# A decoder step's input projection: 21 weight tiles for 23, with the rope key columns spread by a 0/1 product

## The chip, the cores and the metric

The kernel runs on one core of a Trainium2 chip. The metric is the device time of one execution in microseconds; three runs are given for the kernel before, and their median counts. A profile of one execution stands beside them. The engines are TensorE (PE; its weight loads are PEld), VectorE (DVE), ScalarE (ACT), GpSimd (POOL) and SyncE (SP); an engine's name with a q is its queue of DMA issues.

## The reference, cut to what matters

The reference is one inference step of a two-layer hybrid decoder over 512 prompt tokens and 32 sample tokens (8 sequences of 4), 544 columns in all. Each layer begins with one combined projection, whose columns are split among three kinds of heads:

```python
proj = x @ lw["w_in"]                     # (544, 1024) @ (1024, 2680)
(z, xbc, dt_raw, q_raw, k_raw, v_raw, r_raw, g_lr, cq, ckv, kr) = jnp.split(proj, ...)
...
log_a = jax.nn.log_sigmoid(g_lr @ lw["gla_gate_w"] + lw["gla_gate_b"]) / GLA_TAU
...
x1, x2 = kr[..., :16], kr[..., 16:]
k_rope = concatenate([x1 * cos - x2 * sin, x1 * sin + x2 * cos])
```

Widths: z 512, xbc 1024, dt 8, q and k 128 each, v and r 256 each, the gate rows g_lr 16, cq 192, ckv 128 and the rope keys kr 32. Behind the projection come the state-space heads (SSD), the gated linear attention (GLA), the latent attention (MLA, the only one to use kr), the output projection, a norm, the feed-forward part and a second norm.

## The kernel before, in words

Everything is kept transposed: features on the 128 partitions, the 544 tokens along the row, split into two halves of 272 columns (HALF) because a PSUM bank holds 512 numbers. The layers are a hardware loop over L (line 499); inside it each stage is a block with one instruction list per engine, and a block ends with a barrier of all engines.

The change lies in the first block, the input projection (lines 500 to 692). Its weights come from HBM in loads of up to 256 columns of w_in into a ring of four slots (RING); PROJ_LOADS (lines 251 to 259) lists the pieces of each of 12 loads, PROJ_TILES (lines 261 to 270) cuts them into 23 tiles of 128 columns, in the order in which TensorE takes them: 12 tiles of z and xbc, 6 of q, k, v and r, then the first 128 columns of cq, ckv, the rope keys four times over (J_KR), the rope keys with their halves swapped four times over (J_KS), and last a mixed tile (J_MISC): the other 64 columns of cq, a block of 32 from C_DT on and a block of 32 from C_G on, of which the first 8 and the first 16 are wanted. The two key tiles are one load of twelve pieces, the mixed tile one of three.

Weights and activations are split into a high part (rounded to fp32r) and a low part (the rest), and a product is w_high x_high + w_high x_low + w_low x_high: 8 blocks of rows x 3 x 2 halves = 48 products a tile (split_product, lines 336 to 346). For tile i ScalarE rounds the weights (high_weights, line 320), GpSimd subtracts (low_weights, line 324), TensorE multiplies into one of three pairs of PSUM banks (line 343), and ScalarE copies the result to proj (line 641) or, for xbc, to the convolution's rows (lines 634 to 638). ScalarE's order is written out (lines 628 to 653): wait for product i, round tile i + 2, copy tile i; VectorE and ScalarE do the convolution beside it. On TensorE, line 587 puts the transposes of the parameter rows behind tile 3 and line 589 those of a small weight behind tile 8.

After the last tile TensorE waits for all copies (line 592) and transposes the convolution's last rows (lines 593 to 602); ScalarE copies them (lines 655 to 662), SP stores them and starts four w_out loads (lines 557 to 564), and the block ends.

SP's order in the block: two ring loads, 16 rows of parameters, the third ring load, small weights (lines 536 to 551; the gate's weight gw is line 539), the fourth, then the others, each when the product that last used its slot is done (slot_free, lines 309 to 312).

Later users: the SSD block transposes dt out of rows 64 to 95 of the mixed tile (line 748), the GLA block multiplies gw by the 16 gate rows (line 1134, two halves, K = 16), the MLA block squares and scales the cq rows and multiplies the keys by cos and the swapped keys by sin (lines 1541, 1588, 1589, 1595). mlaw, where gw lies, is written over by the low weights of later stages in every layer.

The constants are one host-made array (const_layout, host_constants), loaded once at the start (line 426). Its sel has, for each of four heads, a 0/1 matrix that spreads 32 rows to four groups of 32.

## Time and profile before

| | us |
|---|---|
| median of 3 runs | 2667.15 |
| lowest, highest run | 2656.22, 2682.72 |
| span of the profiled execution, first to last instruction | 2667.4 |
| its mean granted TensorE clock | 0.844 |

The profiled execution has no other time than its span; the span is 0.25 us over the median of the runs. In the rows, a start time counts from the span's first instruction. A row of the timeline has start, duration, engine, line, operation, written tile <- read tiles, shapes, and x the number of instructions merged; in brackets is the time for which the engine had been idle before it and what ended that. A granted clock of 1.00 is the upper of TensorE's two levels (2.4 GHz), 0.50 the lower (1.2 GHz).

### The profile page before, as it was taken

To read this page: it belongs to the slowest core of one execution; us is meant where nothing else is said; L and a number is where in the kernel's file an instruction comes from. 1 tells how busy PE (TensorE), PEld (TensorE's weight loads), DVE (VectorE), ACT (ScalarE), POOL (GpSimd) and SP (SyncE) were. 2 spreads that over 40 slices of the span, in tenths; PEclk is the share of its full clock that TensorE was granted. 3 is DMA by queue.
4 is the path that set the end of the run, shared out by engine and by line. 5 is a ranking of instruction groups with operands and counts; after the bars stand their busy time and mean duration, and the time that the engine had idled before them with its cause. 6 is when DMAs were issued, how large, how long until landed. Compare 5 with 4: busy or idle time off the path is not lost. (4 is left out here: it accounts for less than half of the span.)

```text
span 2667.4 us, 38846 instructions
## 1 busy us (share of the span) xinstructions
PE 2310.9 (87%) x16043; PEld 2092.2 (78%) x16043; DVE 916.7 (34%) x1506; ACT 813.8 (31%) x1471; POOL 657.1 (25%) x332
## 2 busy tenths in 40 slices
PE   4996677899987999989969785688998989999896
PEld 3995363498977999989859763446997889999896
DVE  2415562211123243335425067421111314343453
ACT  4322323222214222233344232323221232222334
POOL 0332040000022234334323223200000323434341
PEclk7997565778788999999989875657797999999998
DMA  3323102022111232222033301201230102222220
GB/s 109 106 40 97 40 5 84 7 73 96 63 36 41 79 96 94 77 84 88 24 109 80 104 5 36 84 6 40 80 119 4 64 31 90 95 94 95 66 80 34
DMA packets 168754, 177.14 MB, mean 66 GB/s; under 512 B 47199, under 2 KB 151303, under 8 KB 166341
## 3 DMA queue, kind: packets, MB, share of 16 engines
q1 hardware_dynamic: 163884, 132.51, 16.3%
q0 software_dynamic: 4608, 41.95, 4.3%
q8 instruction: 111, 1.82, 0.3%
q10 hardware_dynamic: 100, 0.46, 0.1%
q14 instruction: 51, 0.41, 0.1%
HBM read 166.04 MB, written 8.86 MB: 66 GB/s over the span
## 5 line engine op out<-in xcount | busy, mean ns | idle before, releaser
L324 POOL TENSOR_TENSOR w_low<-ring,w_high 128x1024 fp32r<-128x1024 f32 x120 | 291.2, 2427 | 678.2 <-ACT w_high L320 678.2
L343 PE MATMUL ps<-x_high,w_high 128*128 128x272 f32 x1664 | 347.0, 290 | 28.3 <-DVE x_low L334 22.3
L343 PE MATMUL ps<-x_high,w_low 128*128 128x272 f32 x1664 | 346.0, 289 | 0.0
L343 PE MATMUL ps<-x_low,w_high 128*128 128x272 f32 x1664 | 345.7, 289 | 0.0
L320 ACT ACTIVATE w_high<-ring 128x1024 fp32r<-128x1024 f32 x166 | 174.8, 1055 | 544.5 <-PE ps L343 489.2
L343 PEld LDWEIGHTS ps<-x_high,w_high 128*128 128x128 f32 x1664 | 262.8, 190 | 30.0 <-DVE x_low L334 23.2
L343 PEld LDWEIGHTS ps<-x_high,w_low 128*128 128x128 f32 x1664 | 262.4, 189 | 0.0
L343 PEld LDWEIGHTS ps<-x_low,w_high 128*128 128x128 f32 x1664 | 262.3, 189 | 0.0
L343 PE MATMUL ps<-x_high_in,w_high 128*128 128x272 f32 x736 | 154.3, 291 | 45.5 <-POOL w_low_in L324 45.5
L2183 DVE TENSOR_SCALAR arena<-arena,parb 128x560 f32<-128x560 f32 x44 | 84.6, 1922 | 277.3 <-ACT arena L2131 277.3
L1708 PE MATMUL ps<-xc 128*128 128x16 f32 x1024 | 176.6, 308 | 0.6
L324 POOL TENSOR_TENSOR w_low_in<-ring,w_high 128x1024 fp32r<-128x1024 f32 x46 | 109.9, 2390 | 271.7 <-ACT w_high L320 271.7
L1708 PEld LDWEIGHTS ps<-xc 128*128 128x128 f32 x1024 | 172.4, 254 | 2.3 <-ACT xc L1799 2.3
L2271 DVE TENSOR_TENSOR hidden_low<-big,hidden_high 128x544 fp32r<-128x544 f32 x88 | 122.1, 1394 | 138.5 <-ACT hidden_high L2238 138.5
L2258 PE MATMUL ps<-hidden_high,w_high 128*128 128x272 f32 x704 | 148.1, 292 | 12.7 <-DVE hidden_low L2271 11.9
L2245 POOL TENSOR_TENSOR w_low<-ring,w_high 128x512 fp32r<-128x512 f32 x88 | 117.3, 1336 | 169.2 <-ACT w_high L2237 169.2
L343 PEld LDWEIGHTS ps<-x_high_in,w_high 128*128 128x128 f32 x736 | 117.0, 190 | 46.5 <-POOL w_low_in L324 46.4
L343 PE MATMUL ps<-x_high_in,w_low_in 128*128 128x272 f32 x736 | 153.4, 290 | 0.0
L343 PE MATMUL ps<-x_low_in,w_high 128*128 128x272 f32 x736 | 152.9, 290 | 0.0
L2258 PE MATMUL ps<-hidden_low,w_high 128*128 128x272 f32 x704 | 147.5, 291 | 0.0
L2258 PE MATMUL ps<-hidden_high,w_low 128*128 128x272 f32 x704 | 147.1, 290 | 0.0
L2258 PEld LDWEIGHTS ps<-hidden_high,w_high 128*128 128x128 f32 x704 | 112.7, 192 | 13.6 <-POOL w_low L2245 12.5
(376 smaller groups left out, 3959.8 us busy)
## 6 DMA issues: line engine op xcount, KB each, us to landing
ring<-in_ffn_w_up SPq DMA_DIRECT2D x44, 1024.0 KB, 5.3
ring<-in_ffn_w_down SPq DMA_DIRECT2D x20, 1024.0 KB, 5.1
ring<-in_w_in SPq DMA_DIRECT2D x18, 1024.0 KB, 5.4
ring<-in_w_out SPq DMA_DIRECT2D x8, 1024.0 KB, 9.0
ring<-in_ple_w_gate SPq DMA_DIRECT2D x8, 1024.0 KB, 5.0
big<-in_state_ssm SPq DMA_DIRECT2D x16, 256.0 KB, 5.1
out_ssm_sample<-big SPq DMA_DIRECT2D x4, 1024.0 KB
arena<-in_x_prompt SPq DMA_DIRECT2D x1, 2048.0 KB
```

The costliest lines, as they stand in the source:

```text
L320: act.activation(wh[:, i % 2], ring[:, n % RING, :, c0:c0 + P], ACT.Copy).then_inc(s_high, 1)
L324: pool.tensor_tensor(low[:, i % 2], ring[:, n % RING, :, c0:c0 + P], wh[:, i % 2].bitcast(F32), ALU.subtract).then_inc(s_low, 1)
L343: last = pe.matmul(ps[:, b + h, 0:HALF], w[:, i % 2, k, :], x[:, k, h * HALF:(h + 1) * HALF], start=(k == 0 and x is x_high and w is wh), ...
L1708: last = pe.matmul(ps[:, sb_, 16 * t:16 * t + 16], kvT[:, n % 4, q * P:(q + 1) * P], qls[:, b].rearrange("p h l -> p (h l)"), start=False, ...
L2183: dve.tensor_scalar(c2, ab[:, i, 0:AO], pcol(0), pcol(3), ALU.mult, ALU.add)
L2245: pool.tensor_tensor(wld[:, s % 4], down_slot(LD_DOWN + i)[:, r_], whd[:, s % 4].bitcast(F32), ALU.subtract).then_inc(s_wl, 1)
L2258: last = pe.matmul(ps[:, 2 * m + h, 0:HALF], w[:, s % 4, m * P:(m + 1) * P], x[:, s % 4, h * HALF:(h + 1) * HALF], start=(k == 0 and w is ...
L2271: dve.tensor_tensor(hl[:, s % 4], hT[:, k], hh[:, s % 4].bitcast(F32), ALU.subtract).then_inc(s_hl, 1)
```

## The change

The rope key columns are loaded once, as rows 96 to 127 of the mixed tile. The two key tiles are gone; in their place a float32 product of a 32-row 0/1 matrix with these rows writes them four times over (matrix: sel for head 3) and swapped four times over (matrix: a new constant, kswap) into PSUM, and ScalarE copies them to the places where they were. The mixed tile moves ahead of the cq and ckv tiles; the first spread product stands behind the cq tile's product, the second behind the last one. The gate rows move from row 96 to row 72, which is no start for a product's rows, so that the gate product takes rows 64 to 95 and its weight has zeros for the rows that aren't gate rows: VectorE zeroes 32 rows of the weight, and SP's load of it waits for that.

```diff
-M_DT, M_G = 64, 96
+M_DT, M_G, M_KR = 64, 72, 96
...
-              ("eps_rms", 1), ("quarter", 1), ("blk64", 128), ("mean", 128), ("pgsel", 128)]
+              ("eps_rms", 1), ("quarter", 1), ("blk64", 128), ("mean", 128), ("pgsel", 128), ("kswap", 128)]
...
+    kswap = np.zeros((P, P), np.float32)
+    for rep in range(4):
+        for d in range(RD):
+            kswap[M_KR + (d + RD // 2) % RD, 32 * rep + d] = 1.0
+    put("kswap", kswap)
...
+        PROJ_LOADS.append([(0, C_CQ + 128, 64), (M_DT, C_DT, 8), (M_G, C_G, 16), (M_G + 16, C_G, 8),
+                           (M_KR, C_KR, RD)])
         PROJ_LOADS.append([(0, C_CQ, 128), (128, C_CKV, 128)])
-        PROJ_LOADS.append([(32 * r, C_KR, 32) for r in range(4)]
-                          + [(128 + 32 * r + 16 * h, C_KR + 16 * (1 - h), 16) for r in range(4) for h in range(2)])
-        PROJ_LOADS.append([(0, C_CQ + 128, 64), (64, C_DT, 32), (96, C_G, 32)])
...
-        PROJ_TILES += [(9, 0, 128, "c", J_CQ), (9, 128, 128, "c", J_CKV), (10, 0, 128, "c", J_KR),
-                       (10, 128, 128, "c", J_KS), (11, 0, 128, "c", J_MISC)]
+        PROJ_TILES += [(9, 0, 128, "c", J_MISC), (10, 0, 128, "c", J_CQ), (10, 128, 128, "c", J_CKV)]
...
-        N_IN, LD_OUT, LD_GATE, LD_PROJ, LD_UP, LD_DOWN = 12, 12, 16, 20, 21, 43
+        N_IN, LD_OUT, LD_GATE, LD_PROJ, LD_UP, LD_DOWN = 11, 11, 15, 19, 20, 42
...
-        gw = mlaw[M_G:M_G + 16, 1792:1920]
+        gw = mlaw[M_DT:M_DT + 32, 1792:1920]
...
-                    e.dma_start(gw, a["gla_gate_w"][L]).then_inc(s_w, 16)
+                    e.wait_ge(s_gz, 1)
+                    e.dma_start(mlaw[M_G:M_G + 16, 1792:1920], a["gla_gate_w"][L]).then_inc(s_w, 16)
...
+                    def spread_rope_keys(swapped):
+
+                        e.wait_ge(s_kept, N_PROJ - 2)
+                        by = C("kswap") if swapped else sel[:, 3, :]
+                        for h in range(2):
+                            last = pe.matmul(ps[:, (6, 0)[swapped] + h, 0:HALF], by[M_KR:M_KR + RD, :],
+                                             proj[M_KR:M_KR + RD, J_MISC, h * HALF:(h + 1) * HALF],
+                                             start=True, stop=True)
+                        last.then_inc(s_rep, 1)
...
                         if i == 8:
                             transposed_uk()
+                        if i >= N_PROJ - 2:
+                            spread_rope_keys(i - (N_PROJ - 2))
 
                     e.wait_ge(s_kept, N_PROJ)
+                    e.wait_ge(s_repk, 2)
...
+                        if i >= N_PROJ - 2:
+                            swapped = i - (N_PROJ - 2)
+                            e.wait_ge(s_rep, swapped + 1)
+                            act.activation(two(proj[:, (J_KR, J_KS)[swapped]]), halves((6, 0)[swapped]), ACT.Copy
+                                           ).then_inc(s_repk, 1)
...
                 @block.vector
                 def _(e):
+                    dve.memset(gw, 0.0).then_inc(s_gz, 1)
                     low_x(e, xl_in, xT, xh_in, s_xh, s_xl)
...
-                        last = pe.matmul(ps[:, h, 0:HALF], gw, proj[M_G:M_G + 16, J_MISC, h * HALF:(h + 1) * HALF],
+                        last = pe.matmul(ps[:, h, 0:HALF], gw, proj[M_DT:M_DT + 32, J_MISC, h * HALF:(h + 1) * HALF],
                                          start=True, stop=True)
```

## Rows read from the trace of the kernel before

**Rows 1.** The page, busy time of each engine (share of the span) x instructions.

```profile
PE 2310.9 (87%) x16043; PEld 2092.2 (78%) x16043; DVE 916.7 (34%) x1506; ACT 813.8 (31%) x1471; POOL 657.1 (25%) x332
```

**Rows 2.** Line 343 on TensorE, projection of each layer: from:to, length, busy, clock, DMA share, GB/s; one group.

```profile
63.10:204.20 141.10, 140.54 (x1104) 0.99 0.32 77
1366.30:1507.70 141.40, 140.85 (x1104) 0.99 0.31 76
...
L343 PE MATMUL ps<-x_high_in,w_low_in 128*128 128x272 f32 x736 | 153.4, 290 | 0.0
```

**Rows 3.** Timeline of ScalarE and GpSimd in the last tiles of layer 0's projection.

```profile
168.15 1.06 ACT L320 ACTIVATE w_high<-ring 128x1024 fp32r<-128x1024 f32 x1 [4.44 <-PE ps L343]
...
180.18 1.06 ACT L320 ACTIVATE w_high<-ring 128x1024 fp32r<-128x1024 f32 x1 [4.44 <-PE ps L343]
...
186.19 1.06 ACT L320 ACTIVATE w_high<-ring 128x1024 fp32r<-128x1024 f32 x1 [4.44 <-PE ps L343]
187.16 0.61 ACT L641 ACTIVATE big<-ps 128x544 f32<-128x544 f32 x1
187.33 2.39 POOL L324 TENSOR_TENSOR w_low_in<-ring,w_high 128x1024 fp32r<-128x1024 f32 x1 [3.62 <-ACT w_high L320]
...
192.20 1.06 ACT L320 ACTIVATE w_high<-ring 128x1024 fp32r<-128x1024 f32 x1 [4.44 <-PE ps L343]
```

**Rows 4.** Timeline of the end of layer 0's projection, to the next block's first product.

```profile
203.78 0.41 PE L343 MATMUL ps<-x_high_in,w_low_in 128*128 128x272 f32 x2
204.23 0.62 ACT L641 ACTIVATE big<-ps 128x544 f32<-128x544 f32 x1 [5.38 <-PE ps L343]
204.90 0.74 PEld L594 LDWEIGHTS ps<-cst,big 128*3 128x3 f32 x8 [0.93 <-ACT big L641]
...
209.07 5.49 SPq L245 DMA_DIRECT2D ring<-in_w_out  x4
...
215.01 0.66 PE L748 MATMUL ps<-cst,big 32*128 32x32 f32 x5 [8.20 <-PEq L512]
```

**Rows 5.** Float32 products of 272 columns: a group over the whole span, and a timeline row.

```profile
L2009 PE MATMUL ps<-big,ring 128*128 128x272 f32 x128 | 29.7, 392 | 0.0
...
313.45 2.15 PE L1134 MATMUL ps<-big,mlaw 16*128 16x272 f32 x4 [6.13 <-PEq L728]
```

**Rows 6.** SP's issues of the twelve-piece load, and slices: from:to, length, clock, DMA share, GB/s.

```profile
150.24 1.82 SPq L245 DMA_DIRECT2D ring<-in_w_in  x3
...
140.00:143.00 3.00, 1.00 1.12 306
...
158.00:161.00 3.00, 1.00 0.93 81
161.00:164.00 3.00, 1.00 0.44 51
```

**Rows 7.** Timeline of layer 0's start: VectorE's first work, SP's load of the gate weight.

```profile
54.54 5.17 DVE L334 TENSOR_TENSOR x_low_in<-xT,x_high_in 128x544 fp32r<-128x544 f32 x8 [3.37 <-ACT x_high_in L329]
...
64.45 0.33 SPq L539 DMA_DIRECT2D mlaw<-in_gla_gate_w  x1
```

**Rows 8.** The constants' load (KB, median us to landing), and TensorE's first work in the timeline.

```profile
cst<-in_consts SPq DMA_DIRECT2D x1, 1695.5 KB, 7.0
...
13.74 6.65 PE L459 MATMUL ps<-cst,arena 128*128 128x128 f32 x40 [13.74 <-DMA arena<-in_x_sample]
```

**Rows 9.** Timeline, the same two points in layer 0 and in layer 1.

```profile
63.11 0.82 PE L343 MATMUL ps<-x_high_in,w_high 128*128 128x272 f32 x2 [20.39 <-POOL w_low_in L324]
...
1344.77 5.62 ACT L414 ACTIVATE xT<-xT,par 128x544 f32<-128x544 f32 x8 [0.85 <-DVE xT L393]
...
1366.31 0.82 PE L343 MATMUL ps<-x_high_in,w_high 128*128 128x272 f32 x2 [25.14 <-POOL w_low_in L324]
...
2649.15 5.62 ACT L414 ACTIVATE xT<-xT,par 128x544 f32<-128x544 f32 x8 [0.85 <-DVE xT L393]
```

More of the change, by code:

```diff
@@ L509, in build @@
             craw = arena[:, 4096:4288].rearrange("p (k r) -> p k r", k=KD)
-            s_craw = sem("convrows_packed")
+            s_craw, s_gz = sem("convrows_packed"), sem("gate_rows_zeroed")
+            s_rep, s_repk = sem("rope_keys_spread"), sem("rope_keys_spread_kept")
             s_wh, s_wl, s_xh, s_xl = (sem(f"in_{n}") for n in ("w_high", "w_low", "x_high", "x_low"))
```

## The prediction

> **What bounds the kernel now.** I read the share of each engine first, then the projection stage by itself, then its last microseconds, and last the queues that feed it. TensorE is busy for 87% of the span and every other engine for 34% or less [rows 1], but the share is a mean over stages, so what a weight tile is worth has to be read where the tiles stand. In the input projection TensorE is busy for 140.54 of 141.10 us in layer 0 and 140.85 of 141.40 us in layer 1, at a granted clock of 0.99 [rows 2], that is, at the upper of its two levels for all but the first microseconds. The row of the products has a mean of 290 ns for one [rows 2]; that is no step, since neighbours overlap. The step is read from who waits for whom: ScalarE starts to round tile after tile at 180.18, 186.19 and 192.20 us, 6.01 us apart, and each time had sat idle 4.44 us until a product was done; its copy out of PSUM (0.61 us) and GpSimd's 2.39 us for the low part both end long before the next tile is asked for [rows 3]. So one tile is 48 products in 6.01 us (125 ns each), and here TensorE alone sets the pace.
>
> The end of the stage is a chain: the last product ends at about 204.19 us, ScalarE copies it (204.23 to 204.85), TensorE starts the transposes of the convolution rows at 204.90, ScalarE copies these, SP then sends four w_out loads from 209.07 for 5.49 us, and only behind the stage's barrier does TensorE go on, at 215.01 [rows 4]. What lengthens the time from the last product to the first transpose lengthens the kernel.
>
> **The change, part by part.** The sum is made against the profiled span, 2667.4 us; the median of the three runs is 2667.15, 0.25 below it, and the same difference is taken from it.
>
> *Two tiles fewer.* 96 products, two weight roundings, two subtractions and two copies go in each of two layers. Their ScalarE and GpSimd work lies beside TensorE now, so its going is worth nothing by itself; the gain is TensorE's: 4 x 6.01 = 24.04 us. The tiles in question are the ones rounded at 180.18 and 186.19 us, and their step is that of the others [rows 3]. After their going the next thing late is still TensorE: ScalarE's and GpSimd's chain for a tile is 1.06 + 2.39 = 3.45 us of the 6.01.
>
> *The first spread product* (two halves) stands between the products of the last two tiles. It waits for the mixed tile's copy, which is in PSUM one whole tile (6.01 us) earlier and takes 0.61 us, so the wait is over on arrival. Queued behind it on TensorE is the last tile's product: its price is a full addition. One float32 product of 272 columns is two records. The nearest row is the float32 product of the gate projection of the embeddings, 128 records in 29.7 us at the full clock, 0.232 us a record [rows 5]; four records make 0.93 us. Upper bound: the gate product of 16 rows, four records in 2.15 us, at the lower clock [rows 5]. Lower bound: two products at the projection's own 125 ns, 0.25 us. I take 0.93, since the row has the same kind, columns and clock; it has 128 rows in place of 32, and the 16-row one shows no gain from fewer rows (2.15 us at half the clock would be 1.08 at the full one). Its copy by ScalarE (0.61 us) lies in ScalarE's 4.44 us of idle time and costs nothing; if that cover were gone it would cost 0.61 a layer.
>
> *The second spread product* follows the last tile and waits for nothing that is late, as the same copy serves it. It is on the chain of the stage's end: 0.93 us of product, then 0.04 us to ScalarE, 0.61 us of copy and 0.05 us to the transposes make 1.63 us after the last product, where the copy and the transposes take 204.90 - 204.19 = 0.71 now. The last tile's own copy (0.62 us) lies beside the product. Added: 0.92 us a layer; bounds 0.25 and 2.15 by the same rows. Behind the new wait on the two copies stand the transposes, ScalarE's copies, SP's stores and four loads, and everybody at the barrier: it is paid in full.
>
> *The loads.* The twelve-piece load (keys and swapped keys) and the three-piece one go, a five-piece one comes. SP issues the twelve pieces from 150.24 us, and the traffic behind them has fallen off in the slice that ends at 164; in between it was 81 GB/s in 158 to 161 us, beside 306 in 140 to 143 us for a tile with rows of 1 KB [rows 6]. So twelve small pieces took about 12 us and held nobody, and five take an estimated 5. The new load takes the place of the one in rows 6 that ran at 140 to 143 us, so it can start at about 138 (product 12 frees its slot), and its first tile is rounded at 168.15 [rows 3]: 30 us, 25 of them to spare. Cost nothing.
>
> *Zeroing of the gate's rows.* VectorE clears 32 x 128 ahead of the low parts, while it waits for ScalarE's first rounding until 54.54 us; SP gets to the gate's load at 64.45, ten microseconds behind [rows 7]. Behind this wait on SP stand the small weights and the ring's fourth load. Nothing, unless the clearing came ten microseconds late. The gate's product has 32 rows in place of 16 at the same columns: nothing, by the rows of 16 and of 128.
>
> *Constants.* 128 more columns are 64 KB on top of 1695.5 KB that land in 7.0 us; TensorE starts at 13.74 us behind x, on the same queue [rows 8]. In proportion that is 7.0 x 64 / 1695.5 = 0.26 us, at the 306 GB/s of rows 6 0.21; I take 0.2, with 0 and 0.3 as ends.
>
> Sum: -24.04 + 2 x (0.93 + 0.92) + 0.2 = -20.1 us. By the low bounds -23.0, by the high ones -24.04 + 8.6 + 0.3 = -15.2. Forecast 2667.15 - 20.1 = **2647.0 us**, 0.75% less. A measurement of this kernel can tell about 1% from no change, so this comes out as within 1%, faster.
>
> **The rivals.**
>
> *The scatter or the later stages carry it over 1%.* The runs of before lie from 2656.22 to 2682.72, 10.9 below and 15.6 above the median, and nothing in the program differs between them. For it: both layers run the same instructions, and the time from the first projection product to the last bias of the second norm is 1344.77 - 63.11 = 1281.66 in layer 0 and 2649.15 - 1366.31 = 1282.84 in layer 1 [rows 9], so the same work at another moment moves by 1.2 us inside one execution, and by more between executions. Against it: that is small beside what is wanted, and has no sign. A draw as low as the lowest of before gives 2647.0 - 10.9 = 2636, below the bound of 2640.5. The Trainium skill (TensorE: Matmul & The Clock Gate, section "What's actually happening") says that the moment at which the clock rises is not tied to the kernel and differs from run to run. By that rule alone each later stage may gain or lose a little when it is moved forward; the 1.2 us of rows 9 agree with an effect of that size.
>
> *The spread goes the slow way.* If the four records run at the lower level of the clock or the copies at the end line up behind one another, both spreads cost 2.15 us each and the copy 0.61 on top: -24.04 + 2 x (4.3 + 0.6) + 0.3 = -13.9, so 2653. For it: the only float32 product with few rows in the trace is that slow [rows 5]. Against it: there TensorE had been idle for six microseconds, here it comes from 120 us at the full clock.
>
> *The mixed tile's load is late, and the change is a loss.* The mixed tile comes three tiles before the end and its five pieces are rows of 32 to 256 bytes; if they land late, ScalarE cannot round the tile and TensorE stands. It begins to cost when the five pieces take more than 30 us and undoes the whole gain at 30 + 10 = 40 us in each layer; at 46 us the kernel would be 2 x 6 = 12 us slower, 2679. Against it: twelve such pieces took 12 us [rows 6]. The Trainium skill (DMA: Bandwidth & Descriptors, the table at its head) states that a transfer of under 512 bytes is written by read-modify-write, which speaks against cutting a load so; by that rule all five pieces would be slow, as rows 6 agree (81 GB/s beside 306), and it still doesn't reach 30 us.
>
> *The stage isn't TensorE's.* If the loads or GpSimd set the step, two tiles fewer would give nothing: 2667 + 4 = 2671. Rows 3 exclude it almost wholly.
>
> **How the numbers follow.** Forecast as worked out, with its bounds 2644 to 2652: 0.63. Carried past 1%: 0.25. Slow spread: 0.07. Late load: 0.03. No gain: 0.02. The forecast's own band widened by the runs' scatter gives low 2636 (the second case's time) and high 2660 (2647 plus most of the 15.6 above the median); about 2 in 10 is left out. Faster by over 1%: 0.25. Slower by over 1%: the late load, 0.03. Within 1%: the rest, 0.72.
>
> **What would show it.** In the profile after, ScalarE's roundings stay 6.01 us apart and number 21 a layer; the first projection product to the last tile's copy is shorter by 2 x 6.01 - 0.93 = 11.1 us; that copy's start to the first conv-row transpose grows from 0.67 to about 1.6 us; the transposes to the next stage's first product stay at 10.1 us; the later stages keep their lengths within a microsecond or two. Wrong would be: a gap at the mixed tile with a DMA as releaser, four spread records taking over 1.2 us, a copy out of PSUM that starts more than 0.1 us behind its product, or a later stage that takes back several microseconds.

## The result, and the profile after

The kernel after takes 2634.86 us in the median of twelve runs (2622.99 to 2648.93). The kernel before, run beside it twelve times, takes 2655.03 us (2640.60 to 2682.72); the ratio is 0.9922 [0.9897, 0.9947]. Ratios and intervals, here and below, leave out runs of more than 1.5% above the fastest of the same kernel; medians and ranges hold all runs. That is 20.2 us less (0.78%), where 20.1 were forecast, and yet the time itself lies 12.1 us below the forecast 2647.0 and 1.1 below the low end 2636.0. Both have to be explained: why the difference came out, and why the level did not.

The profiled execution after spans 2636.7 us, 30.7 less than the one before. The page's share of each engine, to be read beside [rows 1]:

```profile
PE 2278.1 (86%) x15867; PEld 2055.1 (78%) x15867; DVE 917.3 (35%) x1508; ACT 810.4 (31%) x1467; POOL 647.5 (25%) x328
```

The counts are those of the change: TensorE has 176 products fewer (two layers of 96 less 8 of the spreads), GpSimd four subtractions fewer, VectorE two clears more. Next the timeline of layer 0: its start, then the last two tiles and the end of the projection (start, duration, engine, line; in brackets the idle time before and what ended it). After the change L323 rounds weights, L346 is the projection's product, L592 the spread, L659 the tile copy, L668 the spread's copy, L612 the first conv-row transpose, L250 SP's loads and L772 the next block's first product.

```profile
13.58 2.79 PE L462 MATMUL ps<-cst,arena 128*128 128x128 f32 x12 [13.58 <-DMA arena<-in_x_sample]
...
53.91 0.17 DVE L697 MEMSET mlaw<- 32x128 f32 x1 [2.71 <-PEq L172]
54.57 5.17 DVE L337 TENSOR_TENSOR x_low_in<-xT,x_high_in 128x544 fp32r<-128x544 f32 x8 [0.50 <-ACT x_high_in L332]
...
62.80 0.82 PE L346 MATMUL ps<-x_high_in,w_high 128*128 128x272 f32 x2 [20.05 <-POOL w_low_in L327]
...
180.00 1.06 ACT L323 ACTIVATE w_high<-ring 128x1024 fp32r<-128x1024 f32 x1 [4.44 <-PE ps L346]
...
185.90 1.18 PE L592 MATMUL ps<-big,cst 32*128 32x272 f32 x4
186.01 0.62 ACT L659 ACTIVATE big<-ps 128x544 f32<-128x544 f32 x1 [4.44 <-PE ps L346]
187.01 0.52 PE L346 MATMUL ps<-x_high_in,w_high 128*128 128x272 f32 x2
187.12 0.62 ACT L668 ACTIVATE big<-ps 128x544 f32<-128x544 f32 x1 [0.48 <-PE ps L592]
...
193.21 1.18 PE L592 MATMUL ps<-big,cst 32*128 32x272 f32 x4
193.32 0.62 ACT L659 ACTIVATE big<-ps 128x544 f32<-128x544 f32 x1 [5.57 <-PE ps L346]
194.43 0.62 ACT L668 ACTIVATE big<-ps 128x544 f32<-128x544 f32 x1 [0.48 <-PE ps L592]
195.20 1.03 PE L612 MATMUL ps<-cst,big 128*3 128x128 f32 x8 [0.80 <-ACT big L668]
...
199.37 5.89 SPq L250 DMA_DIRECT2D ring<-in_w_out  x4
...
206.07 0.66 PE L772 MATMUL ps<-cst,big 32*128 32x32 f32 x5 [8.97 <-PEq L516]
```

Four things are to be seen. ScalarE still idles 4.44 us in front of a rounding and a tile copy until TensorE is done, as in [rows 3]: TensorE still sets the pace. Between the last two tile copies lie 193.32 - 186.01 = 7.31 us where a tile step is 6.01: the first spread costs 1.30 us. From the last tile's copy to the first transpose lie 195.20 - 193.32 = 1.88 us, where [rows 4] has 204.90 - 204.23 = 0.67: the second spread costs 1.21 us. And the clear of the gate rows (0.17 us) ends before VectorE's first real work, which starts at 54.57 as it did at 54.54 [rows 7].

The loads, in slices of 3 us (from:to, length, busy time of PE, PEld, DVE, ACT and POOL, granted clock, DMA share, GB/s), and below them the cached attention of the sample tokens in layer 0 and in layer 1, from its first product (line 1682) to the copy of its result (line 1836), to which the experiments lead:

```profile
138.00:141.00 3.00, 3.00 (x26) 3.00 (x26) 1.83 (x2) 2.24 (x6) 1.95 (x1) 1.00 0.46 93
141.00:144.00 3.00, 3.00 (x27) 3.00 (x26) 2.78 (x4) 0.08 (x1) 0.45 (x1) 1.00 0.83 72
144.00:147.00 3.00, 3.00 (x27) 3.00 (x26) 0.41 (x1) 2.13 (x4) 1.94 (x1) 1.00 0.10 15
...
517.40:743.80 226.40, 220.19 (x1572) 199.57 (x1572) 29.34 (x74) 55.17 (x111) 11.26 (x12) 0.80 0.20 70
1804.20:2030.60 226.40, 220.19 (x1572) 199.58 (x1572) 29.33 (x74) 55.18 (x111) 11.25 (x12) 0.80 0.20 70
```

The five small pieces are in by 147, some 20 us ahead of their tile, and TensorE is busy throughout. The constants' row:

```profile
cst<-in_consts SPq DMA_DIRECT2D x1, 1759.5 KB, 7.0
```

They still land in 7.0 us, and TensorE starts at 13.58 where it was 13.74 [rows 8]: the longer constants cost nothing that can be seen.

Where the 30.7 us went: from the first projection product to the next block's first product layer 0 takes 206.07 - 62.80 = 143.27 us, where it was 215.01 - 63.11 = 151.90 [rows 2 to 4], 8.6 less; layer 1 takes 9.7 less (142.8 for 152.5). That makes 18.3. The program's start gives 0.3, and that is no part of the change: the first projection product stands at 59.5 to 63.6 us in the profiles of this record, whatever the kernel. The rest lies in a stage that the change does not touch. Its rows in the profile of the kernel before, with the same columns as above:

```profile
527.60:759.90 232.30, 226.13 (x1572) 205.12 (x1572) 29.33 (x74) 55.12 (x111) 11.28 (x12) 0.77 0.19 69
1831.40:2063.80 232.40, 226.17 (x1572) 205.19 (x1572) 29.33 (x74) 55.18 (x111) 11.28 (x12) 0.77 0.19 69
```

The same 1572 products take 226.40 us in place of 232.3, and 12 us are gone in two layers, at a granted clock of 0.80 for 0.77. 18.3 + 0.3 + 11.9 = 30.5 of the 30.7. So the profiles show a change worth 18.3 us and a stage that happened to go faster; the experiments ask whether that second part belongs to the change.

### The profile page after: what moved, and what is told of

The parts are those of the page before. It is cut to its first block and busy times, and to the rows that moved or that the text cites. A ratio compares the mean times of both kernels' runs of the same rounds, so it can differ in the third digit from the quotient of the medians.

```text
span 2636.7 us, 38446 instructions
## 1 busy us (share of the span) xinstructions
PE 2278.1 (86%) x15867; PEld 2055.1 (78%) x15867; DVE 917.3 (35%) x1508; ACT 810.4 (31%) x1467; POOL 647.5 (25%) x328
## 5 line engine op out<-in xcount | busy, mean ns | idle before, releaser
L346 PE MATMUL ps<-x_high,w_high 128*128 128x272 f32 x1664 | 346.4, 290 | 28.3 <-DVE x_low L337 22.3
L346 PE MATMUL ps<-x_low,w_high 128*128 128x272 f32 x1664 | 345.7, 289 | 0.0
L346 PE MATMUL ps<-x_high,w_low 128*128 128x272 f32 x1664 | 345.3, 289 | 0.0
L323 ACT ACTIVATE w_high<-ring 128x1024 fp32r<-128x1024 f32 x162 | 170.8, 1056 | 526.6 <-PE ps L346 472.3
L346 PEld LDWEIGHTS ps<-x_high,w_high 128*128 128x128 f32 x1664 | 262.1, 189 | 30.0 <-DVE x_low L337 23.2
L346 PEld LDWEIGHTS ps<-x_low,w_high 128*128 128x128 f32 x1664 | 262.3, 189 | 0.0
L346 PEld LDWEIGHTS ps<-x_high,w_low 128*128 128x128 f32 x1664 | 261.9, 189 | 0.0
L346 PE MATMUL ps<-x_high_in,w_high 128*128 128x272 f32 x672 | 141.3, 292 | 45.4 <-POOL w_low_in L327 45.4
L1732 PE MATMUL ps<-xc 128*128 128x16 f32 x1024 | 169.5, 301 | 0.6
L2295 DVE TENSOR_TENSOR hidden_low<-big,hidden_high 128x544 fp32r<-128x544 f32 x88 | 122.0, 1393 | 138.0 <-ACT hidden_high L2262 138.0
L1732 PEld LDWEIGHTS ps<-xc 128*128 128x128 f32 x1024 | 165.0, 244 | 2.3 <-ACT xc L1823 2.3
L327 POOL TENSOR_TENSOR w_low_in<-ring,w_high 128x1024 fp32r<-128x1024 f32 x42 | 100.3, 2389 | 256.5 <-ACT w_high L323 256.5
L2282 PE MATMUL ps<-hidden_high,w_high 128*128 128x272 f32 x704 | 147.8, 292 | 12.7 <-DVE hidden_low L2295 11.9
L346 PEld LDWEIGHTS ps<-x_high_in,w_high 128*128 128x128 f32 x672 | 106.8, 191 | 47.0 <-POOL w_low_in L327 46.2
L346 PE MATMUL ps<-x_high_in,w_low_in 128*128 128x272 f32 x672 | 139.9, 290 | 0.0
L346 PE MATMUL ps<-x_low_in,w_high 128*128 128x272 f32 x672 | 139.7, 290 | 0.0
```

The source lines that it names most:

```text
L323: act.activation(wh[:, i % 2], ring[:, n % RING, :, c0:c0 + P], ACT.Copy).then_inc(s_high, 1)
L327: pool.tensor_tensor(low[:, i % 2], ring[:, n % RING, :, c0:c0 + P], wh[:, i % 2].bitcast(F32), ALU.subtract).then_inc(s_low, 1)
L346: last = pe.matmul(ps[:, b + h, 0:HALF], w[:, i % 2, k, :], x[:, k, h * HALF:(h + 1) * HALF], start=(k == 0 and x is x_high and w is wh), ...
L1732: last = pe.matmul(ps[:, sb_, 16 * t:16 * t + 16], kvT[:, n % 4, q * P:(q + 1) * P], qls[:, b].rearrange("p h l -> p (h l)"), start=False, ...
L2282: last = pe.matmul(ps[:, 2 * m + h, 0:HALF], w[:, s % 4, m * P:(m + 1) * P], x[:, s % 4, h * HALF:(h + 1) * HALF], start=(k == 0 and w is ...
L2295: dve.tensor_tensor(hl[:, s % 4], hT[:, k], hh[:, s % 4].bitcast(F32), ALU.subtract).then_inc(s_hl, 1)
```

## The experiments

**The two kernels again, and each spread's price.** Two of the first four kernels are unchanged copies, to see what the cached attention does when nothing changes.

> The kernel before, unchanged, once more. Scatter theory: nothing in the program fixes the length of the cached attention (first product of it to the copy of its result, 232.3 and 232.4 us in the two layers of the profile of before, 226.4 in both layers of the profile of after); this profile shows a length that differs from 232 by 2 us or more, with a different granted clock there, and the other stages within 1 us of the first profile. Rival, that the change itself shortens the cached attention: again 232 within 1 us. Time: ratio 1.00, interval about 0.4% to each side.

> The changed kernel, unchanged, once more. Both theories: from the start of a layer's rounding to the copy of the convolution's rows 141 to 142 us as in its first profile (before 151 to 153). Scatter theory: the cached attention differs from 226.4 by 2 us or more, and the ratio is 1 - 19/2655, 0.993, within 0.003. Rival: cached attention 226.4 within 1 us, and the ratio nearer to 0.990 (19 us of the projection and 7 to 11 of the later stages).

Measured: 2654.61 us for the kernel before (ratio 1.0021 [0.9988, 1.0054]) and 2634.52 for the one after (0.9928 [0.9894, 0.9963]), so the difference repeats. The profile of the first, in windows: the whole cached attention of layer 0 and, of TensorE alone, two slices of it, then the same of layer 1 at the same distance from its start.

```profile
525.90:747.50 221.60, 215.37 (x1572) 194.63 (x1572) 29.31 (x74) 55.11 (x112) 11.23 (x12) 0.81 0.20 72
...
529.90:559.90 30.00, 29.27 (x141) 0.50 0.25 88
559.90:585.90 26.00, 25.95 (x232) 1.00 0.18 61
...
1816.10:2055.10 239.00, 232.72 (x1572) 210.28 (x1572) 29.27 (x74) 55.13 (x112) 11.24 (x12) 0.75 0.19 67
...
1820.10:1850.10 30.00, 29.16 (x140) 0.50 0.24 88
1850.10:1876.10 26.00, 26.00 (x146) 0.61 0.00 1
```

One execution of one kernel, the same 1572 products: 221.6 us in layer 0 and 239.0 in layer 1. The 30 us ahead of the two last slices are alike, at the lower level (0.50). Then layer 0 stays at the upper level for 26 us and does 232 products, while layer 1 is at the lower one again for most of them (0.61 in the mean) and does 146. Layer 1 moves less data in that slice (1 GB/s for 61), and TensorE is busy for all of it: it isn't starved, it is slower. In both layers the clock rises between 33 and 34 us behind the stage's start (0.65 and 0.63 in that microsecond); what differs is the fall. The fall in layer 1, TensorE alone:

```profile
1847.10:1853.10 6.00, 6.00 (x44) 0.77 0.00 0
1853.10:1854.10 1.00, 1.00 (x8) 0.58 0.00 0
1854.10:1873.10 19.00, 19.00 (x92) 0.50 0.00 1
```

TensorE is busy for all of the 6 us ahead of the fall, in which the clock had risen, and for all of the 19 us behind it. The kernel after drew 226.4 and 223.0 in its second profile. So the stage's length changes from one layer, and from one execution, to the next without any change of the program, by as much as the change is worth. The other stages were expected within 1 us of the first profile; two were not: the start (2.2 us shorter) and, in layer 0, the stretch from the cached attention to the next layer's first projection product (603.5 us for 606.4). The cached attention is the greatest source of scatter, not the only one.

The third leaves the spreads and their copies out; VectorE clears the keys instead, so the rope keys are missing from the result.

```diff
-                        if i >= N_PROJ - 2:
-                            spread_rope_keys(i - (N_PROJ - 2))
...
-                    e.wait_ge(s_repk, 2)
...
+                    for j in (J_KR, J_KS):
+                        dve.memset(proj[:, j], 0.0).then_inc(s_repk, 1)
```

> The changed kernel without the two spread products and their copies; the rope keys are left out (VectorE writes zeros in their places while it is idle), so only the going of two tiles is left of the change. From the traces: first spread 1.30 us, second 1.21 us a layer, so 5.0 us less than the changed kernel, 24 less than before, ratio 0.991. By the forecast's terms (0.93 and 0.92) 3.7 less. In the profile: step between the last two tiles 6.01 in place of 7.31 us, copy of the last tile to the first transpose 0.67 in place of 1.88.

Measured: 2643.84 us, ratio 0.9961 [0.9927, 0.9995], where less than the kernel after was expected: a miss by the time. Its timeline at the last two tiles, and its cached attention in windows:

```profile
184.01 0.62 ACT L656 ACTIVATE big<-ps 128x544 f32<-128x544 f32 x1 [4.44 <-PE ps L346]
...
190.02 0.62 ACT L656 ACTIVATE big<-ps 128x544 f32<-128x544 f32 x1 [5.38 <-PE ps L346]
...
190.69 1.04 PE L609 MATMUL ps<-cst,big 128*3 128x128 f32 x8 [0.71 <-ACT big L656]
```

```profile
512.00:764.60 252.60, 246.42 (x1572) 223.41 (x1572) 29.24 (x74) 55.11 (x111) 11.24 (x12) 0.71 0.18 63
1822.70:2047.60 224.90, 218.64 (x1572) 198.63 (x1572) 29.26 (x74) 55.19 (x112) 11.23 (x12) 0.80 0.20 71
```

By the rows the spreads' prices are confirmed: the step is 190.02 - 184.01 = 6.01 again and the end 0.67, so 1.30 and 1.21 us a layer were the spreads. By the time they are drowned: layer 0's cached attention took 252.6 us, 26 more than in the profile after.

The fourth puts both spreads behind the conv-row transposes, into banks that are free there, and their copies behind ScalarE's conv-row copies.

```diff
-                        e.wait_ge(s_kept, N_PROJ - 2)
+                        e.wait_ge(s_kept, N_PROJ)
...
-                            last = pe.matmul(ps[:, (6, 0)[swapped] + h, 0:HALF], by[M_KR:M_KR + RD, :],
+                            last = pe.matmul(ps[:, (2, 4)[swapped] + h, 0:HALF], by[M_KR:M_KR + RD, :],
...
-                        if i >= N_PROJ - 2:
-                            spread_rope_keys(i - (N_PROJ - 2))
...
                     last.then_inc(s_rtr, 1)
+                    for swapped in range(2):
+                        spread_rope_keys(swapped)
```

> Both spread products moved behind the last transposes of the convolution rows, their copies behind the copies of these rows, beside SP's four w_out loads (5.5 to 5.9 us in which the block waits for SP alone). If SP's issue ends the block there, both are free: the same 5.0 us less than the changed kernel as without them, ratio 0.991 to before, and the next block starts when SP has issued, not when ScalarE has copied. If the barrier waits for ScalarE instead, the copies would show as the last thing before it and the gain would be under 3 us.

Measured: 2647.29 us, ratio 0.9956 [0.9921, 0.9992]. Its timeline at the end of the block:

```profile
195.43 2.10 PE L592 MATMUL ps<-big,cst 32*128 32x272 f32 x8
...
197.56 0.62 ACT L682 ACTIVATE big<-ps 128x544 f32<-128x544 f32 x1 [0.29 <-PE ps L592]
197.76 5.80 SPq L250 DMA_DIRECT2D ring<-in_w_out  x4
...
204.38 0.65 PE L771 MATMUL ps<-cst,big 32*128 32x32 f32 x5 [6.86 <-PEq L516]
```

Product and copies end at 198.18, SP's four loads at 203.56: the spreads are hidden behind SP, and it is SP's 5.80 us for which the next block waits. The time again doesn't show it: a second miss, as 0.991 was expected.

**The same kernels once more, and SP's loads.** With the cached attention suspected, the three kernels of the change were run a second time, beside one that moves SP's four w_out loads ahead of its wait for the conv rows, on top of the late spread.

```diff
-                    e.wait_ge(s_rev, 4)
-                    store(e, o["ssm_conv_prompt"][L, 0], crow_p)
...
                     for n in range(LD_OUT, LD_OUT + RING):
...
+                    e.wait_ge(s_rev, 4)
+                    store(e, o["ssm_conv_prompt"][L, 0], crow_p)
```

> The changed kernel a third time, beside the two others on the same chip. Both: ratio 0.993 within 0.004, median 18 to 20 us under before. In the profile the stage from rounding to the copy of the convolution rows 141 to 142 us in each layer; the cached attention anywhere from 221 to 253.

> The changed kernel without its spread products, once more (the rope keys are left out). Its first twelve runs had a median 9 us over the changed kernel's, though its projection stage is 2.4 us a layer shorter. Draw theory (the clock's pattern in the cached attention is drawn anew in every layer of every run, 221 to 253 us so far, and the earlier 9 us were an unlucky draw): median 5 us under the changed kernel's now, within 6. Rival (a kernel without the products gets a worse pattern systematically): again 5 to 15 us over it, and a lower granted clock.

> The version with the spread products behind the convolution rows, once more. Draw theory: 5 us under the changed kernel, within 6. Rival: again 5 to 15 us over it, with more runs above 2650 than the changed kernel has.

> As the late spread, and SP's four w_out loads are started before the wait for the convolution's rows, each when its slot is free, in place of behind their stores. If the block waits for SP's issue alone, the time from the convolution rows' copy to the next block's first product falls from 10.7 to about 5 us a layer, 11 us less than the late spread in all, the clock's draws apart. If the barrier is set by ScalarE or by the stores, under 2 us a layer. The shorter pause may also keep TensorE's clock up at the start of the next block (0.50 there now).

Measured: after 2638.66 us (0.9928 [0.9891, 0.9964]), no spread 2643.63 (0.9926 [0.9888, 0.9965]), late spread 2662.03 over six runs from 2617.51 to 2673.02, five of them above 2658, for which there is no ratio, early loads 2628.67 (0.9855 [0.9794, 0.9915], six runs). The late spread's second profile has 255.8 and 242.8 us of cached attention, its first had 230.5 and 223.1; the no-spread kernel's has 223.1 and 224.8 where its first had 252.6 and 224.9. The longest of them:

```profile
514.00:769.80 255.80, 249.60 (x1572) 226.00 (x1572) 29.29 (x74) 55.17 (x111) 11.23 (x12) 0.70 0.17 62
```

So no kernel has one fixed pattern. But the draw theory's own forecast failed twice: each of the two kernels was to lie 5 us under the kernel after, within 6, and they lay 5.0 and 23.4 over it. In the rows each does save what it should, as from the first projection product to the next block's first product the late spread takes 140.6 to 140.9 us in these two profiles, the no-spread kernel 140.7 to 141.6 and the kernel after 142.8 to 144.2 in its three. What the medians lose again lies behind that stage, and whether these kernels only drew badly or have worse odds is not settled. Early loads, in the timeline at the end of the block:

```profile
194.41 2.02 ACT L678 ACTIVATE mixT<-ps 3x512 f32<-3x512 f32 x4 [0.64 <-PE ps L609]
...
197.00 0.33 SPq L244 DMA_DIRECT2D out_ssm_conv_sample<-mixT  x1
197.31 0.62 ACT L682 ACTIVATE big<-ps 128x544 f32<-128x544 f32 x1 [0.29 <-PE ps L592]
...
198.79 0.43 PE L771 MATMUL ps<-cst,big 32*128 32x32 f32 x5 [1.52 <-PEq L516]
```

From ScalarE's conv-row copy to the next block's first product it takes 198.79 - 194.41 = 4.4 us, where the kernel after takes 206.07 - 196.27 = 9.8. SP's loads were the last link of the chain of [rows 4], and taking them off it gives back 5.4 us a layer. With the hidden spreads the stage and the way to the next block's first product take 135.3 to 135.5 us in all four layers profiled, 15.2 us less in two layers than in the first profile of the kernel after.

**Does a later start of the cached attention change its draw?** If the clock's pattern hangs on when things happen, then a pause that adds nothing but time should move the stage's length, and not in proportion. In the kernel after, VectorE clears a scratch tile once, near the beginning of the cached attention, while TensorE waits for it: 512, 1024 or 2048 columns.

```diff
                     e.wait_ge(s_nw, 1)
+                    dve.memset(xcr[:, 0:1024], 0.0)
+                    e.drain()
                     dve.tensor_tensor(Snew, ps[0:NS, 1, 0:P], C("newmask", NS), ALU.add).then_inc(s_nwk, 1)
```

> The changed kernel with one more clearing by VectorE (128 x 512, about 0.5 us, scratch that is written over later) ahead of the first mask sum of the cached attention, for which TensorE waits: everything after it comes about 0.5 us later in that stage, with the same work. Program alone: 1 us in two layers, median 2638, within 4. If the odds of the clock's pattern hang on where the stage's work stands against the moment at which the clock rises, the median moves by more than 5 us, either way, and the cached attention's lengths in the profile come from another set than 223, 226, 227 and 243.

> The same with 128 x 1024, about 0.9 us. Program alone: 2 us, median 2639, within 4. Odds by position: moved by more than 5 us either way, and not in step with the half microsecond.

> The same with 128 x 2048, about 1.8 us. Program alone: 4 us, median 2641, within 4. Odds by position: off that by more than 5 us either way.

> The late spread with the early w_out loads once more, on another draw of runs. The stage's end again 5.4 us in place of 10.7; by the program 5 us from the hidden spread products and 11 from the loads under the changed kernel, 2621, if the clock's draws are those of the changed kernel; the first six runs had 2629.

Measured, in the median: 0.5 us of pause 2650.07 (0.9944 [0.9910, 0.9977]), 0.9 us 2665.53 (1.0025 [0.9997, 1.0053]), 1.8 us 2641.39 (0.9912 [0.9876, 0.9949]). Expected from the program alone were 2638, 2639 and 2641. All 36 runs of the kernel after have a median of 2636.9, and 13, 29 and 4.5 us lie between; but the kernel before, run beside the pauses, had 2661.24 where it had 2655.03 at first, so the ratios are the fairer measure. Against the 0.9922 to 0.9928 of the kernel after the pauses cost by ratio an estimated 5, 26 and -4 us. Only the 0.9 us is clear of the intervals: all its twelve runs lie at 2659.83 or above, where 35 of the 36 of the kernel after lie under 2655. The costs aren't in order of length, and that one is some 14 times the time that the pause adds in two layers. The clear and TensorE's wait for it, and the cached attention in both layers, with 0.9 us:

```profile
518.44 0.91 DVE L1843 MEMSET xc<- 128x1024 f32 x1 [7.25 <-PE ps L1689]
...
519.95 1.11 PE L1700 MATMUL ps<-cst,big 128*128 128x128 f32 x4 [1.80 <-DVE xc L1845]
...
516.00:754.70 238.70, 231.33 (x1572) 210.12 (x1572) 30.22 (x75) 55.20 (x112) 11.26 (x12) 0.76 0.19 67
1816.50:2055.10 238.60, 231.29 (x1572) 209.72 (x1572) 30.23 (x75) 55.15 (x111) 11.26 (x12) 0.76 0.19 67
```

And with 1.8 us:

```profile
516.90:745.30 228.40, 219.67 (x1572) 198.88 (x1572) 31.07 (x75) 54.92 (x111) 11.28 (x12) 0.80 0.20 70
1807.10:2035.50 228.40, 219.69 (x1572) 198.89 (x1572) 31.07 (x75) 54.96 (x111) 11.26 (x12) 0.80 0.20 70
```

238.7 and 238.6 us against 226.4 twice after: 24.5 us, against a median that rose by 26 to 29. So a pause of under a microsecond at the beginning of the stage, with the same products behind it, changes which patterns it draws, and that moves the whole kernel by more than the change does. Whether it does so by the later start or by TensorE's longer idle time (1.80 us at this point, 0.68 without a pause) these runs don't separate. The early loads were run a second time beside them: 2620.92 us, 0.9872 [0.9822, 0.9921], where 2621 was expected.

**The change on equal patterns.** The 1.8 us pause gave 228.4 us in both layers and eight of its eleven runs within 2640.24 to 2643.00. So the same pause was put into the kernel before, and into the no-spread (again without rope keys) and the late-spread one, to compare them on one pattern.

```diff
                     e.wait_ge(s_nw, 1)
+                    dve.memset(xcr[:, 0:2048], 0.0)
+                    e.drain()
```

> The changed kernel with the pause of 1.8 us again, as the control on this chip: median 2641 within 3, standard deviation about 4, cached attention 228.4 in both layers.

> The kernel before with the same pause. If the pause fixes the pattern here too (228.4 in both layers), the difference to steady_after is the program's share of the change alone: 18.8 us by the rows (2660), 20.1 by the forecast (2661), with little scatter. If the draw belongs to the change, the cached attention is another length here and the difference is off 19 by more than 5.

> Without the spread products (rope keys left out), with the same pause. If the earlier loss was the draw: 5 us under steady_after (2636; 3.7 by the forecast's terms), cached attention 228.4. If a kernel without them is slower by its own doing: not under steady_after.

> The spread products behind the convolution rows, with the same pause: like steady_no_spread, 5 us under steady_after, if they are hidden and the draw is fixed; otherwise above 2641 with a wide scatter.

Measured, in this order: 2641.58 us (0.9921 [0.9888, 0.9954]), 2668.18 (1.0029 [0.9993, 1.0065]), 2642.41 (0.9920 [0.9887, 0.9953]) and 2640.21 (0.9921 [0.9887, 0.9956]). It was only half a success: the first is the 1.8 us kernel over again, and its profile has 243.1 us in one layer and 228.4 in the other, so the pause makes one pattern likely, not certain. The times missed what was expected: the kernel before was to lie 19 us over the kernel after, within 5, and lies 26.6 over it, with six of its twelve runs from 2673 to 2689, for which there is no profile; the kernel without the spreads and the one with late spreads were to lie 5 us under the kernel after, and lie 0.8 over and 1.4 under it. So the medians leave open whether the change shifts the odds, and what follows rests on single executions. The kernel before with the pause, in windows:

```profile
527.90:756.30 228.40, 219.69 (x1572) 198.85 (x1572) 31.10 (x75) 54.92 (x111) 11.23 (x12) 0.80 0.20 70
1828.40:2056.80 228.40, 219.67 (x1572) 198.86 (x1572) 31.09 (x75) 54.91 (x111) 11.22 (x12) 0.80 0.20 70
```

And the no-spread one (the late spread's profile has 228.5 and 229.3 us):

```profile
512.80:741.20 228.40, 219.68 (x1572) 198.33 (x1572) 31.07 (x75) 54.94 (x111) 11.24 (x12) 0.80 0.20 70
1799.60:2028.00 228.40, 219.69 (x1572) 198.34 (x1572) 31.06 (x75) 54.94 (x111) 11.23 (x12) 0.80 0.20 70
```

These two profiles and the one of the 1.8 us pause above have the cached attention equal to a tenth of a microsecond, and so can be laid side by side. Before to after: spans 2660.6 and 2639.1, 21.5 apart, of which 3.35 lie ahead of the first projection product (63.19 and 59.84 us in these two executions); 18.2 are left, 17.4 of them in the projection stages, beside 18.3 read from the first pair of profiles. Without the spreads: 2632.3, 6.8 less than with them, where the rows say 2 x (1.30 + 1.21) = 5.0; the projection stages themselves are 2.53 us a layer shorter; the other 1.8 lies behind them and is not accounted for. The medians, which mix patterns, put no difference between the kernels with and without spreads. That one change of 5 us can be had from rows, and not from twelve runs of this kernel, is what this set shows.

**What the scatter is made of.** All profiles of the two kernels, those with a pause among them, taken apart into the two cached attentions and the rest of the span (us):

| kernel | profiles | span | both cached attentions | rest of the span |
|---|---|---|---|---|
| before | 3 | 2658.8 to 2667.4 | 456.8 to 464.7 | 2198.2 to 2203.8 |
| after | 7 | 2631.0 to 2662.7 | 449.4 to 479.3 | 2179.8 to 2183.9 |

The span of the kernel after moves by 31.7 us, its rest by 4.1: the scatter sits in the cached attention. The rests differ by 19.6 us in the mean, of which 1.6 lie ahead of the first projection product. Without these, 18.0 us are left, beside the 18.3 of the first pair; the projection stages alone differ by 17.5 in the mean.

## Why the prediction was right or wrong

**Right: what bounds the stage, and the size of the gain.** The tile step of 6.01 us stayed, and two tiles a layer went at that price; the difference of the medians, 20.2 us, agrees with the forecast 20.1, though the interval (14 to 27 us) would have taken in much. That they agree to 0.1 us is luck: by rows the change is worth 18.3 us, 1.8 less than forecast, and the terms that were off are these:

- *The first spread*, "four records make 0.93 us": 1.30. The records are 1.18 us from first start to last end, and the rest of the step goes at the change back to the projection's products (0.52 us for the first two of them, where two take 0.41 in [rows 4]). The second, "Added: 0.92 us a layer": 1.21. Both were sized by the mean of a long row of equal products [rows 5], where one overlaps the next (392 ns each, 0.232 us a record); the last of four has no such neighbour. Both lie inside the bounds 0.25 and 2.15.
- "The transposes to the next stage's first product stay at 10.1 us": 10.9 in layer 0 (206.07 - 195.20) and 10.5 in layer 1, where the kernel before has 10.4. Of the 0.76 us in layer 0 SP's loads are 0.40 (5.89 for 5.49); the other 0.36 lie between their end and the next product, and the cause is open.
- *Constants*, "I take 0.2": nothing seen. *Gate rows* and *loads*: nothing, as forecast, with the cover that was named. The gate product takes 2.15 us with 32 rows as it did with 16 [rows 5], both at the lower clock (0.50). The five pieces, "an estimated 5" us, were issued at 138.0 and took up to 9, of 30 to spare. The gate product after the change:

```profile
304.00 2.15 PE L1158 MATMUL ps<-big,mlaw 32*128 32x272 f32 x4 [6.14 <-PEq L752]
```

The three rivals about this stage fell: the spreads weren't slow (1.18 us, and the copies start 0.04 us behind them), the small pieces landed 20 us early, and the stage is TensorE's.

**Wrong: the level.** The step that failed is the weighing of the first rival: "the same work at another moment moves by 1.2 us inside one execution" [rows 9], and on it "the later stages keep their lengths within a microsecond or two". The profile of before had drawn 232.3 and 232.4 us of cached attention in its two layers, one pattern twice, and by that chance its two layers agreed. The same kernel profiled again has 221.6 and 239.0. The spread of that stage over all profiles, 221.6 to 255.8 us, makes most of the scatter of the runs; it isn't "small beside what is wanted", it is larger than the gain.

From that came the second failing step, the base: "Forecast 2667.15 - 20.1". This term was 12.1 us too high, and that is the whole miss of the time. The median of three runs and the profiled span agreed to 0.25 us and seemed to confirm each other (not quite like with like: in every later profile the execution's time is about 1.8 us over its span, as 2638.48 to 2636.7), but both were draws from the upper half: twelve runs of before have a median of 2655.03, and 2655.03 - 20.1 = 2634.9, which is what the kernel after measured. "A draw as low as the lowest of before gives 2647.0 - 10.9 = 2636" took the lowest of three runs for the low end; the lowest of twelve is 2640.60, 15.6 us under that.

What could have been read: the granted clock of the cached attention was 0.77 with TensorE busy for 226 of 232 us, a stage between two levels. The clock alone, from 0.70 in the slowest to 0.81 in the quickest profile of that stage, makes some 34 us a layer: length times granted clock is 179 to 183 us in every row shown (255.80 x 0.70 = 179, 221.60 x 0.81 = 179, 228.40 x 0.80 = 183), so the length follows the clock to within 2%, and little is left for any other cause. The Trainium skill (TensorE: Matmul & The Clock Gate, section "What's actually happening") says that the moment of the clock's rise differs from run to run; the prediction cited it, and took its size from the one pair of layers that happened to agree. The trace agrees in that the clock's course differs between two layers of one execution, by 17.4 us; there, though, the rise came at the same place, and the fall didn't.

**What stays open.** What sets the moment of each fall inside the stage was not found. That a pause at its beginning moves the pattern is shown by the 0.9 us; that the place in time does it is not. That the change itself shifts the odds, apart from its 18.3 us, is neither shown nor excluded: the kernels with the rope keys at other places drew short and long patterns alike, but their medians lay over the forecast of the draw theory each time, and the two kernels with the same pause lie further apart than the rows say.

**A faster version.** The late spread with early loads measured 0.9855 [0.9794, 0.9915] and 0.9872 [0.9822, 0.9921] of the kernel before. Its 5.4 us a layer are seen in the rows; its medians, 2628.67 and 2620.92, lie under all three of the kernel after (2634.52 to 2638.66), though the intervals of the two overlap, and its profiles drew 223.0 to 232.4 us of cached attention; what of it is the program's own stays with the rows: 15.2 us under the kernel after in the projection stages, some 10.7 of them from the loads, and 9.7 by the span without the cached attentions, in the mean of its two profiles.

## What to carry to other kernels

Before a sum is set on a base, look for a stage in which TensorE is busy throughout at a granted clock between its two levels, and compare it over several executions: its scatter belongs to the range, and two layers of one profile that agree prove nothing. A change that is worth less than that scatter is judged by its own stage's rows, or on executions that drew the same pattern. And a few products set between others cost more here than the mean of a long row of their kind (1.2 to 1.3 us for 0.93), while the loads that SP issued ahead of the block's barrier counted almost in full (5.4 us a layer of 5.5 to 5.9).

## What the runs showed of the hardware

The clock fell while TensorE was fully busy: 6.00 us of 6.00 ahead of the fall, and 26.00 us of 26.00 around it at a granted clock of 0.61, with 1 GB/s of DMA traffic, in the second layer of the second profile of before. The Trainium skill (TensorE: Matmul & The Clock Gate, section "HAM oscillation — how this bites in real kernels") tells of a clock that falls in the middle of a kernel because TensorE stands idle for its data; no such wait stands in this row, so here the trace goes further than the page. A pause of 0.91 us, once in each layer, moved the kernel by an estimated 26 us (by ratio; 29 by the median), and one of 1.76 us by nothing that is clear of the intervals.

A float32 product of 32 rows took no less than one of 128: 1.18 us for four records, where four of the 128-row kind in [rows 5] make 0.93 in a long row; and at the lower clock four took 2.15 us with 16 rows and with 32. Five pieces of a weight tile with rows of 32 to 256 bytes were in within 9 us of their slot coming free, beside twelve in about 12 [rows 6].
